# Attention to the memory by three one-pass products, with ScalarE scaling the probabilities

## The chip, the cores and the metric

The kernel runs on one core of a Trainium2 chip. The metric is the device time of one execution in microseconds; lower is better. Engines: PE (TensorE), DVE (VectorE), ACT (ScalarE), POOL (GpSimd) and SP (SyncE, which here only issues DMAs). Each engine works through its own instructions in the order in which they are written, and waits on semaphores.

## What is computed

Two transformer blocks in a row on 512 tokens of width 1024. The change touches one sublayer of the second block: attention from the tokens to a memory of 256 rows, with 4 heads of 256 channels.

```python
def memory_cross_attention(h, mem_n, w_mem_q, w_mem_kv, w_mem_o):
    q = jnp.einsum("bsd,de->bse", h, w_mem_q).reshape(B, S, MEM_HEADS, MEM_HEAD_DIM)
    kv = jnp.einsum("bmd,de->bme", mem_n, w_mem_kv)
    k = kv[..., :D_MODEL].reshape(B, M, MEM_HEADS, MEM_HEAD_DIM)
    v = kv[..., D_MODEL:].reshape(B, M, MEM_HEADS, MEM_HEAD_DIM)
    s = jnp.einsum("bshd,bmhd->bhsm", q, k).astype(jnp.float32) * (MEM_HEAD_DIM ** -0.5)
    p = jax.nn.softmax(s, axis=-1).astype(v.dtype)
    o = jnp.einsum("bhsm,bmhd->bshd", p, v).reshape(B, S, D_MODEL)
    return jnp.einsum("bse,ed->bsd", o, w_mem_o)
```

The rest of the two blocks (the projections, two other attentions, convolutions and two feed-forward parts) is the same before and after.

## The kernel before

**Products.** Nearly all matrix products are made of three one-pass products of float32r operands (`mm3`, L909 to L912): an operand is split into a high part and a remainder, and high x high, low x high and high x low are added up in the bank. POOL splits the weights slab by slab (`split`, L752 to L758: a high copy, L756, and the subtraction, L758, 128x2048 each). The high part of an activation is a copy by ACT out of the bank, its remainder a subtraction by DVE. A product of plain float32 operands is one call, which the trace shows as two instructions. In the attention to the memory the scores (`scoresm`, L1423) and the values (`valuesm`, L1441) are plain float32 products, and the transposes of the probabilities (`turnm`, L1432) are plain products with an identity.

**Staging.** The keys and values of the memory, `mem_k` and `mem_v`, are made in earlier parts of the kernel and copied out of their banks by ACT (L1588). They were computed from `mt_hi` and `mt_lo`, the split of the normalized memory, which nothing reads after that. The queries are projected in 8 banks, the first four in two halves of 256 tokens, the last four 512 wide from two slabs of weights; ACT copies each bank to `qm` (L1634, called at L1968) and thereby frees it. PE waits for all 8 banks (L1451) and for a DMA that brought back half of `mem_k` (L1452).

**The order of the stage.** `ATTM_ORDER` is written out by `head_order` (L224): z0, z1, t0, z2, t1, o0, z3, t2, o1, t3, o2, o3. Here z is a head's scores (4 tiles of 128 tokens by 256 keys), t its transposes (2 banks of 128 keys by 512 tokens), o its values (2 banks of 128 channels by 512 tokens). PE, ACT and DVE each walk through this same list. The 32 tiles go round the 8 banks in turn.

- DVE, at z (L2489 to L2501): for each of 4 tiles the maximum (L2494) and its product with minus the scale (L2495, through the helper at L2059); then for each tile the reciprocal of the sum (helper at L2065) and the product of the probabilities by it (L2501, also L2059). At o: the remainder of the head's output (`lo_of_head`, L2242, helper at L2050).
- ACT, at z (L1870 to L1878): for each tile the exponential with its sum (L1876), which frees the bank. At t: the copy of the transposed probabilities to `ptm` or `ptm_odd` (L1885), which frees the bank. At o: the high part of the output (`split_head`, L1673, at L1678).
- PE, at t, waits for DVE's probabilities (L1433), and at o for ACT's copies (L1442).

Before the stage ACT loads the table for the exponential (L1966). POOL splits the slabs of the query and output projections in one loop (L862). After the stage PE goes on with the output projection from `mem_o` (L1455).

Of the kernel before, what the change touches and what calls it, by code (L numbers as in the profile page):

```python
# [20 lines left out]
ALU = mybir.AluOpType  # L21
# [274 lines left out]
def build(nc, A, out):  # L296
    with ExitStack() as ctx:
# [3 lines left out]
        def sem(name):  # L301
            return ctx.enter_context(nc.semaphore(name))
# [98 lines left out]
        with ExitStack() as lend:  # L401
            dn_lo = sb("dn_lo", [P, 7, D], F32R, where=lend)
            p1_sum = sb("p1_sum", [P, 2, T], where=lend)
        mem_k = sb("mem_k", [P, DC, NM])
        mem_v = sb("mem_v", [P, MT, D])
        mt_hi = sb("mt_hi", [P, DC, NM], F32R)
# [25 lines left out]
        ph = ExitStack()  # L432
        qm = sb("qm", [P, DC, T], where=ph)
        pm = sb("pm", [P, 2, NT, NM], where=ph)
        ptm = sb("ptm", [P, MT, T], where=ph)
        gain5 = sb("gain5", [P, D], where=ph)
        ptm_odd = sb("ptm_odd", [P, MT, T], where=ph)
        ptm_of = (ptm, ptm_odd)
        ph.close()

# [298 lines left out]
        def _(g):  # L739
# [117 lines left out]
            for i in range(2 * NT * (PAIRS - POOL_PAIRS), 2 * NT * PAIRS):  # L857
# [3 lines left out]
                g.tensor_scalar(out, out, smx[:, 2, j, qt:qt + 1], 1.0, ALU.mult, ALU.mult).then_inc(sm_p_pool, 1)  # L861
            split_all(n, S0["ffn"] + 2)  # L862
            g.wait_ge(xn5_ready, NT)
# [29 lines left out]
        def _(pe):  # L893
# [9 lines left out]
            def slab(i=None, per=0):  # L903
# [3 lines left out]
                return n % RING  # L907

            def mm3(o, ah, al, bh, bl, start, stop):  # L909
                inc_free(pe.matmul(o, ah, bh, start=start, stop=False))  # L910
                pe.matmul(o, al, bh, start=False, stop=False)  # L911
                return pe.matmul(o, ah, bl, start=False, stop=stop)  # L912

# [509 lines left out]
            def scoresm(h):  # L1423
                for qt in range(NT):
                    t = Tile(TTM["z", h] + qt)
                    t.wait_free(pe)
                    for c in range(2):
                        ins = pe.matmul(t.ap[:, 0:NM], qm[:, 2 * h + c, qt * P:qt * P + P], mem_k[:, 2 * h + c, :],  # L1428
                                        start=c == 0, stop=c == 1)
                    ins.then_inc(t.full, 1)  # L1430
# [10 lines left out]
            def valuesm(h):  # L1441
                all_taken(range(TTM["t", h], TTM["t", h] + MT))  # L1442
                for c in range(2):
                    t = Tile(TTM["o", h] + c)
                    t.wait_free(pe)
                    for kc in range(MT):
                        ins = pe.matmul(t.ap[:], mem_v[:, kc, h * MHD + c * P:h * MHD + c * P + P], ptm_of[h % 2][:, kc],  # L1447
                                        start=kc == 0, stop=kc == MT - 1)
                    ins.then_inc(t.full, 1)

            all_taken(range(T0["mem_q"], T0["mem_q"] + DC))  # L1451
            pe.wait_ge(k_back, 16)  # L1452
            for what, h in ATTM_ORDER:
# [57 lines left out]
        def _(act):  # L1511
# [356 lines left out]
            def softmax_attention(order, tt, heads, keys, p_of, pt, scale, mb, out_of):  # L1868
                for what, h in order:
                    if what == "z":  # L1870
                        for qt in range(NT):
                            t = Tile(tt["z", h] + qt)
                            act.wait_ge(sm_max, mb + NT * h + qt + 1)
                            if h >= 2 and qt == 0:
                                Tile(tt["t", h - 2] + keys // P - 1).wait_full(act)
                            st.done(act.activation(p_of(h)[:, qt], t.ap[:, 0:keys], ACT.Exp, scale=scale(h, qt),  # L1876
                                                   bias=smx[:, 0, h % 2, qt:qt + 1],
                                                   accum_out=smx[:, 1, h % 2, qt:qt + 1]), tile=t)  # L1878
                    elif what == "t":
                        for kc in range(keys // P):  # L1880
                            t = Tile(tt["t", h] + kc)
                            t.wait_full(act)
                            if h >= 2 and kc == 0:
                                Tile(tt["o", h - 2] + len(out_of(h)) - 1).wait_full(act)
                            st.done(act.copy(pt[h % 2][:, kc], t.ap[:]), tile=t)  # L1885
                    elif what == "m":
                        memory_out(h)
                    else:
                        for c, n in enumerate(out_of(h)):
                            split_head(tt["o", h] + c, ht_hi, h if heads == H1 else None, n)  # L1890
# [74 lines left out]
            act.dma_start(gain5[:], A["norm_ffn_pre_2"].partition_broadcast(P)).then_inc(gain5_loaded, 16)  # L1965
            load_table(ACT.Exp)  # L1966
            for m in range(DC):
                copy_out(T0["mem_q"] + m, qm[:, m])  # L1968
            softmax_attention(ATTM_ORDER, TTM, MH, NM, lambda h: pm[:, h % 2], ptm_of, lambda h, qt: SCM, NT * H1,
                              lambda h: [2 * h, 2 * h + 1])  # L1970
# [71 lines left out]
        def _(v):  # L2042
# [442 lines left out]

            def softmax_attention(order, tiles, heads, keys, p_of, minus_scale, mb, ob, out_of, fill):
                seen = ob
                for what, h in order:
                    if what == "z":  # L2489
                        for qt in range(NT):  # L2490
                            t = Tile(tiles["z", h] + qt)
                            t.wait_full(v)
                            st.after()
                            do(v.tensor_reduce(smx[:, 3, h % 2, qt:qt + 1], t.ap[:, 0:keys], AX_X, ALU.max))  # L2494
                            ts(smx[:, 0, h % 2, qt:qt + 1], smx[:, 3, h % 2, qt:qt + 1], *minus_scale(h, qt), ALU.mult,  # L2495
                               ALU.mult, sem=sm_max)
                        for qt in range(NT):
                            fill()
                            Tile(tiles["z", h] + qt).wait_taken(v)
                            recip(smx[:, 2, h % 2, qt:qt + 1], smx[:, 1, h % 2, qt:qt + 1])  # L2500
                            ts(p_of(h)[:, qt], p_of(h)[:, qt], smx[:, 2, h % 2, qt:qt + 1], None, ALU.mult, sem=sm_p)  # L2501
                    elif what == "o":
# [51 lines left out]
            for c in range(CC):  # L2554
                v.wait_ge(part_hi, CC + DC + c + 1)
                tt(ht_lo[:, c], ay[:, c], ht_hi[:, c].bitcast(F32), ALU.subtract, part_lo)
            post_and_norm(lambda m: post_psum(2, m, T0["w_out2"]), "nt4", col(V_NMEM, 8), ht_hi, ht_lo)
            softmax_attention(ATTM_ORDER, TTM, MH, NM, lambda h: pm[:, h % 2], lambda h, qt: (-SCM, None), NT * H1, 2 * PAIRS,
                              lambda h: [2 * h, 2 * h + 1], lambda: None)
# [173 lines left out]
```

## Time and profile before

| | |
|---|---|
| timed runs | 1483.13 us median of 3 (1480.7 to 1483.78) |
| profiled execution | 1481.8 us |
| its span, first to last instruction | 1480.0 us |
| mean granted clock of PE over the span | 0.998 of full speed |
| PE busy | 1440.3 us, 97% |
| DVE, ACT, POOL busy | 833.5, 552.0, 988.7 us |

The trace is of one execution. Times in it are microseconds from the first instruction. In a row of the timeline or of a group, `out<-in` names the tile written and the tiles read, L is a line of the kernel (often that of a helper), `x16` is the number of instructions; what stands in square brackets, or after a bar, is the idle time of the engine just before and what ended it. Matmuls are pipelined, so the distance of their starts counts, not their durations. PEclk is the granted clock of PE as a share of full speed.

### The profile page before, as it was taken

To read this page: it belongs to the slowest core of one execution; us is meant where nothing else is said; L and a number is where in the kernel's file an instruction comes from. 1 tells how busy PE (TensorE), PEld (TensorE's weight loads), DVE (VectorE), ACT (ScalarE), POOL (GpSimd) and SP (SyncE) were. 2 spreads that over 40 slices of the span, in tenths; PEclk is the share of its full clock that TensorE was granted. 3 is DMA by queue.
4 is the path that set the end of the run, shared out by engine and by line. 5 is a ranking of instruction groups with operands and counts; after the bars stand their busy time and mean duration, and the time that the engine had idled before them with its cause. 6 is when DMAs were issued, how large, how long until landed. Compare 5 with 4: busy or idle time off the path is not lost.

```text
span 1480.0 us, 18618 instructions
## 1 busy us (share of the span) xinstructions
PE 1440.3 (97%) x6987; PEld 1169.2 (79%) x6987; DVE 833.5 (56%) x1302; ACT 552.0 (37%) x1075; POOL 988.7 (67%) x398
## 2 busy tenths in 40 slices
PE   3999999999999999999999999999999999999997
PEld 3888777778888888888898844789789888888886
DVE  6998144443665655566744786441516555465655
ACT  3201134332554434444333386452424523333214
POOL 1867454445678889888567995365154989788653
PEclk9999999999999999999999999999999999999999
DMA  9875221222543332322443200133024323232131
GB/s 346 301 269 211 100 85 58 86 105 95 173 143 111 114 114 93 107 98 73 156 136 100 85 1 1 63 130 122 1 86 143 114 87 113 86 114 86 58 98 73
DMA packets 103385, 167.88 MB, mean 113 GB/s; under 512 B 3917, under 2 KB 61185, under 8 KB 102785
## 3 DMA queue, kind: packets, MB, share of 16 engines
q1 hardware_dynamic: 100176, 160.45, 31.5%
q10 hardware_dynamic: 3121, 6.26, 1.3%
q8 instruction: 56, 0.92, 0.2%
q14 instruction: 32, 0.26, 0.1%
HBM read 161.97 MB, written 4.72 MB: 113 GB/s over the span
## 4 chain that ended last, share of the span: by engine, by line
PE 87%; DVE 8%; ACT 3%; DMA 1%; issue 1%; DVEq 0%; SPq 0%; ACTq 0%
PE bank L910 26%; PE bank L911 26%; PE bank L912 26%; DVE bank L2054 2%; DMA ada_w<-in_w_ada 1%; DVE smx L2514 1%; DVE x L2050 1%; PE bank L1371 1%; PE bank L1428 1%; PE bank L1447 1%; PE bank L1171 1%; DVE bank L2050 1%; ACT junk L1540 1%; PE bank L1194 1%; DVE facc L2050 1%
## 5 line engine op out<-in xcount | busy, mean ns | idle before, releaser
L910 PE MATMUL bank<-ht_hi,w_hi 128*128 128x512 f32 (+1 forms) x1200 | 442.7, 369 | 0.5 <-DVE ht_lo L2050 0.3
L912 PE MATMUL bank<-ht_lo,w_hi 128*128 128x512 f32 (+1 forms) x1200 | 440.0, 367 | 0.0
L911 PE MATMUL bank<-ht_hi,w_lo 128*128 128x512 f32 (+1 forms) x1200 | 440.0, 367 | 0.0
L758 POOL TENSOR_TENSOR w_lo<-w_raw,w_hi 128x2048 fp32r<-128x2048 f32 x83 | 388.7, 4683 | 6.9
L756 POOL TENSOR_SCALAR w_hi<-w_raw 128x2048 fp32r<-128x2048 f32 x83 | 162.3, 1955 | 340.8 <-DMA w_raw<-in_w_in 108.8
L910 PEld LDWEIGHTS bank<-ht_hi,w_hi 128*128 128x128 f32 x1200 | 226.4, 189 | 41.5 <-DVE ht_lo L2050 1.8
L912 PEld LDWEIGHTS bank<-ht_lo,w_hi 128*128 128x128 f32 x1200 | 226.4, 189 | 37.2
L911 PEld LDWEIGHTS bank<-ht_hi,w_lo 128*128 128x128 f32 x1200 | 226.5, 189 | 36.7 <-issue 0.5
L808 POOL TENSOR_TENSOR dn_lo<-dn_raw,dn_hi_all 128x1024 fp32r<-128x1024 f32 x77 | 184.8, 2422 | 49.3 <-ACT dn_hi_all L1738 49.2
L2054 DVE SCALAR_TENSOR_TENSOR uc<-bank,par,uc 128x511 f32<-128x511 f32 x88 | 66.0, 750 | 128.4 <-ACT uc L1992 125.2
L822 POOL TENSOR_TENSOR dn_raw<-dn_raw 128x1024 f32<-128x1024 f32 x44 | 105.9, 2408 | 18.1 <-DMA dn_raw<-in_w_mlp_out 7.3
L910 PE MATMUL bank<-w_hi,ht_hi 128*128 128x512 f32 x256 | 100.4, 392 | 0.2 <-DVE facc L2050 0.2
L1992 ACT ACTIVATE uc<-bank,par 128x512 f32<-128x512 f32 x44 | 34.4, 781 | 176.9 <-PE bank L912 176.8
L912 PE MATMUL bank<-w_lo,ht_hi 128*128 128x512 f32 x256 | 99.7, 389 | 0.0
L911 PE MATMUL bank<-w_hi,ht_lo 128*128 128x512 f32 x256 | 99.6, 389 | 0.0
L2050 DVE TENSOR_TENSOR facc<-bank,facc 128x512 f32<-128x512 f32 x120 | 83.0, 692 | 22.5 <-PE bank L912 14.3
L2054 DVE SCALAR_TENSOR_TENSOR ada_acc<-ada_w,cvec,ada_acc 128x1024 f32<-128x1024 f32 x42 | 79.4, 1890 | 8.3 <-DMA ada_w<-in_w_ada 4.5
L1738 ACT CAST dn_hi_all<-dn_raw 128x1024 fp32r<-128x1024 f32 x77 | 77.1, 1054 | 18.1 <-PE bank L912 15.2
L910 PE MATMUL bank<-dn_hi_all,hf_hi 128*128 128x512 f32 x176 | 68.6, 390 | 0.6 <-issue 0.5
L911 PE MATMUL bank<-dn_hi_all,hf_lo 128*128 128x512 f32 x176 | 68.5, 389 | 0.0
L912 PE MATMUL bank<-dn_lo,hf_hi 128*128 128x512 f32 x176 | 68.5, 389 | 0.0
L2050 DVE TENSOR_TENSOR bank<-bank,hr 128x512 f32<-128x512 f32 x32 | 22.4, 700 | 81.1 <-ACT hr L1751 80.3
(302 smaller groups left out, 2402.7 us busy)
## 6 DMA issues: line engine op xcount, KB each, us to landing
w_raw<-in_w_in SPq DMA_DIRECT2D x27, 1024.0 KB, 5.0
ada_w<-in_w_ada SPq DMA_DIRECT2D x48, 512.0 KB, 7.1
w_raw<-in_w_up SPq DMA_DIRECT2D x22, 1024.0 KB, 4.9
w_raw<-in_w_mlp_in SPq DMA_DIRECT2D x16, 1024.0 KB, 5.6
dn_raw<-in_w_mlp_out SPq DMA_DIRECT2D x28, 512.0 KB, 4.6
w_raw<-in_w_out SPq DMA_DIRECT2D x8, 1024.0 KB, 5.0
w_raw<-in_w_mem_kv SPq DMA_DIRECT2D x8, 1024.0 KB, 5.3
dn_raw<-in_w_down SPq DMA_DIRECT2D x16, 512.0 KB, 5.2
```

Source lines behind the costliest of these rows:

```text
L756: g.tensor_scalar(w_hi[:, r], w_raw[:, r], 1.0, 1.0, ALU.mult, ALU.mult).then_inc(slab_hi, 1)
L758: g.tensor_tensor(w_lo[:, r], w_raw[:, r], w_hi[:, r].bitcast(F32), ALU.subtract).then_inc(slab_split, 1)
L808: g.tensor_tensor(dn_lo[:, w], dn_raw[:, w], dn_hi(w).bitcast(F32), ALU.subtract).then_inc(dn_split, 1)
L822: g.tensor_tensor(dn_raw[:, o], dn_raw[:, a], dn_raw[:, b], ALU.subtract).then_inc(t_made, 1)
L910: inc_free(pe.matmul(o, ah, bh, start=start, stop=False))
L911: pe.matmul(o, al, bh, start=False, stop=False)
L912: return pe.matmul(o, ah, bl, start=False, stop=stop)
L1171: pe.matmul(t.ap[:, 0:W1[qt]], q1[o, p, qt * P:qt * P + P], k1[o, p, 0:W1[qt]], start=True, stop=True).then_inc(t.full, 1)
L1738: st.done(act.copy(dn_hi(w), dn_raw[:, w]), dn_cast)
L1992: st.done(act.activation(uc[:, c], tiles[c].ap[:], ACT.Identity, scale=par[:, p, 2 + g, k:k + 1], bias=par[:, p, 6 + g, k:k + 1]), uc_ready)
L2050: do(v.tensor_tensor(o, a, b, op), sem, tile)
L2054: do(v.scalar_tensor_tensor(out=o, in0=a, scalar=s, in1=b, op0=op0, op1=op1), sem, tile)
```

## The change

The scores and the values of the attention to the memory are computed by three one-pass products (`three`, which `mm3` now also calls). What this needs, and what goes with it:

- ACT casts `mem_k` and `mem_v` to high parts (into the space of `mt_lo` and `mt_hi`) right after the table load; POOL makes their remainders in place, between the third and the fourth slab of the query projection. PE waits for these remainders in place of the DMA.
- ACT writes the queries scaled, as a high part; DVE makes the remainder out of the bank and frees it.
- DVE writes the row maximum negated, in one instruction; the exponential has scale 1.
- DVE writes only the reciprocal of the sums; ACT multiplies the probabilities by it, after the four exponentials of a head.
- ACT's copy of the transposed probabilities is their high part; DVE makes the remainder and frees the bank (a new branch at t in its list).

```diff
@@ buffers @@
+        mem_k_lo = sb("mem_k_lo", [P, DC, NM], F32R)
+        mem_v_lo = sb("mem_v_lo", [P, MT, D], F32R)
...
+        mem_k_hi = mt_lo
+        mem_v_hi = mt_hi[:].rearrange("p (a b) n -> p a (b n)", a=MT)
@@ POOL @@
-            split_all(n, S0["ffn"] + 2)
+            split_all(n, S0["mem_q"] + 3)
+            g.wait_ge(kv_hi, 1)
+            g.tensor_tensor(mem_k_lo[:], mem_k[:], mem_k_hi[:].bitcast(F32), ALU.subtract).then_inc(kv_lo, 1)
+            g.wait_ge(kv_hi, 2)
+            g.tensor_tensor(mem_v_lo[:], mem_v[:], mem_v_hi.bitcast(F32), ALU.subtract).then_inc(kv_lo, 1)
+            split_all(S0["mem_q"] + 3, S0["ffn"] + 2)
@@ PE @@
+            def three(o, ah, al, bh, bl, start, stop):
+                first = pe.matmul(o, ah, bh, start=start, stop=False)
+                pe.matmul(o, al, bh, start=False, stop=False)
+                return first, pe.matmul(o, ah, bl, start=False, stop=stop)
...
-                        ins = pe.matmul(t.ap[:, 0:NM], qm[:, 2 * h + c, qt * P:qt * P + P], mem_k[:, 2 * h + c, :],
-                                        start=c == 0, stop=c == 1)
+                        q = slice(qt * P, qt * P + P)
+                        _, ins = three(t.ap[:, 0:NM], qm_hi[:, 2 * h + c, q], qm_lo[:, 2 * h + c, q],
+                                        mem_k_hi[:, 2 * h + c, :], mem_k_lo[:, 2 * h + c, :], c == 0, c == 1)
...
-                        ins = pe.matmul(t.ap[:], mem_v[:, kc, h * MHD + c * P:h * MHD + c * P + P], ptm_of[h % 2][:, kc],
-                                        start=kc == 0, stop=kc == MT - 1)
+                        d = slice(h * MHD + c * P, h * MHD + c * P + P)
+                        _, ins = three(t.ap[:], mem_v_hi[:, kc, d], mem_v_lo[:, kc, d], ptm_of[h % 2][:, kc],
+                                  ptm_lo[h % 2][:, kc], kc == 0, kc == MT - 1)
...
-            pe.wait_ge(k_back, 16)
+            pe.wait_ge(kv_lo, 2)
@@ ACT @@
+                        for qt in range(NT):
+                            act.wait_ge(pm_inv, NT * h + qt + 1)
+                            st.done(act.activation(p_of(h)[:, qt], p_of(h)[:, qt], ACT.Copy,
+                                                   scale=smx[:, 2, h % 2, qt:qt + 1]), sm_p)
...
-                            st.done(act.copy(pt[h % 2][:, kc], t.ap[:]), tile=t)
+                            st.done(act.copy(pt[h % 2][:, kc], t.ap[:]), ptm_made)
...
+            act.wait_ge(k_back, 16)
+            st.after()
+            st.done(act.copy(mem_k_hi[:], mem_k[:]), kv_hi)
+            st.done(act.copy(mem_v_hi, mem_v[:]), kv_hi)
             for m in range(DC):
-                copy_out(T0["mem_q"] + m, qm[:, m])
-            softmax_attention(ATTM_ORDER, TTM, MH, NM, lambda h: pm[:, h % 2], ptm_of, lambda h, qt: SCM, NT * H1,
+                t = Tile(T0["mem_q"] + m)
+                t.wait_full(act)
+                st.done(act.activation(qm_hi[:, m], t.ap[:], ACT.Copy, scale=SCM), qm_made)
+            softmax_attention(ATTM_ORDER, TTM, MH, NM, lambda h: pm[:, h % 2], ptm_of, lambda h, qt: 1.0, NT * H1,
@@ DVE @@
-                            do(v.tensor_reduce(smx[:, 3, h % 2, qt:qt + 1], t.ap[:, 0:keys], AX_X, ALU.max))
-                            ts(smx[:, 0, h % 2, qt:qt + 1], smx[:, 3, h % 2, qt:qt + 1], *minus_scale(h, qt), ALU.mult,
-                               ALU.mult, sem=sm_max)
+                            do(v.tensor_reduce(smx[:, 0, h % 2, qt:qt + 1], t.ap[:, 0:keys], AX_X, ALU.max, negate=True),
+                               sm_max)
...
-                            recip(smx[:, 2, h % 2, qt:qt + 1], smx[:, 1, h % 2, qt:qt + 1])
-                            ts(p_of(h)[:, qt], p_of(h)[:, qt], smx[:, 2, h % 2, qt:qt + 1], None, ALU.mult, sem=sm_p)
+                            recip(smx[:, 2, h % 2, qt:qt + 1], smx[:, 1, h % 2, qt:qt + 1], pm_inv)
+                    elif what == "t":
+                        for kc in range(MT):
+                            t = Tile(tiles["t", h] + kc)
+                            v.wait_ge(ptm_made, MT * h + kc + 1)
+                            tt(ptm_lo[h % 2][:, kc], t.ap[:], ptm_of[h % 2][:, kc].bitcast(F32), ALU.subtract, tile=t)
...
+            for m in range(DC):
+                v.wait_ge(qm_made, m + 1)
+                t = Tile(T0["mem_q"] + m)
+                stt(qm_lo[:, m], t.ap[:], SCM, qm_hi[:, m].bitcast(F32), ALU.mult, ALU.subtract, tile=t)
```

## Rows read from the trace of the kernel before

**Rows 1.** The page, engines: busy time, share of the span, instructions

```profile
PE 1440.3 (97%) x6987; PEld 1169.2 (79%) x6987; DVE 833.5 (56%) x1302; ACT 552.0 (37%) x1075; POOL 988.7 (67%) x398
```

**Rows 2.** Chain of waits, 1005 to 1090: start us, length us, engine, tile, line

```profile
1042.32 0.59 ACT qm L1634
...
1043.27 7.14 PE bank L1428 x32
1050.41 0.87 PE bank L1438 x8
1051.28 3.46 PE bank L1428 x16
...
1055.61 3.44 PE bank L1447 x8
...
1074.55 0.23 PE bank L910
```

**Rows 3.** Windows, the stage: length, each engine's busy us, PEclk, DMA

```profile
1043.00:1076.00 33.00, 32.73 (x135) 22.97 (x136) 21.79 (x72) 18.32 (x49) 0.26 (x1) 1.00 0.02 1
```

**Rows 4.** Timeline, PE: first and last of 52, then of 34: start, duration

```profile
1005.82 0.28 PE L912 MATMUL bank<-ht_lo,w_hi 128*128 128x256 f32 x1
...
1011.94 0.28 PE L912 MATMUL bank<-ht_lo,w_hi 128*128 128x256 f32 x1
...
1034.42 0.39 PE L912 MATMUL bank<-ht_lo,w_hi 128*128 128x512 f32 x1
...
1041.90 0.39 PE L912 MATMUL bank<-ht_lo,w_hi 128*128 128x512 f32 x1
```

**Rows 5.** Timeline, ACT: exp and copy of a head; the first copy of qm

```profile
1016.22 0.59 ACT L1634 COPY qm<-bank 128x512 f32<-128x512 f32 x1 [8.94 <-PE bank L912]
...
1052.35 0.47 ACT L1876 ACTIVATE pm<-bank,smx 128x256 f32<-128x256 f32 x1 [0.15 <-DVE smx L2059]
...
1052.82 1.06 ACT L1885 COPY ptm<-bank 128x512 f32<-128x512 f32 x2
```

**Rows 6.** Timeline, ACT elsewhere: products by a column, 128 and 512 wide

```profile
810.28 7.71 ACT L1854 ACTIVATE tap_m<-ident,vec 128x128 f32<-128x128 f32 x26
...
867.92 0.71 ACT L1909 ACTIVATE p2c<-p2c,smx 128x512 f32<-128x512 f32 x1
868.53 0.71 ACT L1909 ACTIVATE p2b<-p2b,smx 128x512 f32<-128x512 f32 x1
```

**Rows 7.** Timeline, DVE: product, reciprocal, two remainders, maximum

```profile
1052.62 0.35 DVE L2059 TENSOR_SCALAR pm<-pm,smx 128x256 f32<-128x256 f32 x1
1052.89 0.15 DVE L2065 RECIPROCAL smx<-smx 128x1 f32<-128x1 f32 x1
...
1059.11 1.49 DVE L2050 TENSOR_TENSOR ht_lo<-bank,ht_hi 128x512 fp32r<-128x512 f32 x2
1060.70 0.42 DVE L2494 TENSOR_REDUCE smx<-bank 128x1 f32<-128x256 f32 x1
```

**Rows 8.** Groups by shape, DVE, ACT: busy us, mean ns, idle before

```profile
L2054 DVE SCALAR_TENSOR_TENSOR ay<-bank,ay 128x512 f32<-128x512 f32 x4 | 2.8, 692 | 1.7 <-PE bank L1399 1.6
...
L1743 ACT CAST w_hi<-w_raw 128x2048 fp32r<-128x2048 f32 x14 | 26.9, 1919 | 12.6 <-DMA w_raw<-in_w_mlp_in 12.6
```

**Rows 9.** Timeline, POOL: splits around its idle time

```profile
1002.48 4.62 POOL L758 TENSOR_TENSOR w_lo<-w_raw,w_hi 128x2048 fp32r<-128x2048 f32 x1
...
1019.91 1.92 POOL L756 TENSOR_SCALAR w_hi<-w_raw 128x2048 fp32r<-128x2048 f32 x1 [12.81 <-DMA w_raw<-in_w_mem_q]
```

**Rows 10.** Timeline, a wait of PE on DVE at 1113 to 1115

```profile
1113.48 1.28 DVE L2054 SCALAR_TENSOR_TENSOR xn<-x,stat,gain 128x1024 f32<-128x1024 f32 x1
...
1115.23 1.91 PE L1084 MATMUL bank<-ident,xn 128*128 128x128 f32 x16
```

**Rows 11.** Timeline, PE, then its window (length, PE busy, PEclk, DMA), 171 to 180

```profile
171.52 3.63 PE L1128 MATMUL bank<-ones,ada_acc 128*128 128x1 f32 x32
...
174.00:180.00 6.00, 6.00 (x22) 0.72 0.43 125
```

More of the change, by code:

```diff
@@ L403, in build @@
             p1_sum = sb("p1_sum", [P, 2, T], where=lend)
-        mem_k = sb("mem_k", [P, DC, NM])
-        mem_v = sb("mem_v", [P, MT, D])
+        with ExitStack() as lend:
+            mem_k = sb("mem_k", [P, DC, NM], where=lend)
+            mem_v = sb("mem_v", [P, MT, D], where=lend)
+        mem_k_lo = sb("mem_k_lo", [P, DC, NM], F32R)
+        mem_v_lo = sb("mem_v_lo", [P, MT, D], F32R)
         mt_hi = sb("mt_hi", [P, DC, NM], F32R)
@@ L432, in build @@
         ph = ExitStack()
-        qm = sb("qm", [P, DC, T], where=ph)
+        qm_hi = sb("qm_hi", [P, DC, T], F32R, where=ph)
         pm = sb("pm", [P, 2, NT, NM], where=ph)
-        ptm = sb("ptm", [P, MT, T], where=ph)
+        ptm = sb("ptm", [P, MT, T], F32R, where=ph)
         gain5 = sb("gain5", [P, D], where=ph)
-        ptm_odd = sb("ptm_odd", [P, MT, T], where=ph)
+        ptm_odd = sb("ptm_odd", [P, MT, T], F32R, where=ph)
         ptm_of = (ptm, ptm_odd)
+        qm_lo = sb("qm_lo", [P, DC, T], F32R, where=ph)
+        ptm_lo = [sb(f"ptm_lo{i}", [P, MT, T], F32R, where=ph) for i in range(2)]
+        mem_k_hi = mt_lo
+        mem_v_hi = mt_hi[:].rearrange("p (a b) n -> p a (b n)", a=MT)
         ph.close()
@@ L473, in build @@
         squared, mlp_slab_hi, mlp_hi, mlp_sums = (sem(n) for n in ("squared", "mlp_slab_hi", "mlp_hi", "mlp_sums"))
+        qm_made, ptm_made, kv_hi, kv_lo, pm_inv = (sem(n) for n in ("qm_made", "ptm_made", "kv_hi", "kv_lo", "pm_inv"))
         memory_kept, mt_back, k_back = sem("memory_kept"), sem("mt_back"), sem("k_back")
@@ L907, in slab @@
                 return n % RING
+            def three(o, ah, al, bh, bl, start, stop):
+                first = pe.matmul(o, ah, bh, start=start, stop=False)
+                pe.matmul(o, al, bh, start=False, stop=False)
+                return first, pe.matmul(o, ah, bl, start=False, stop=stop)
             def mm3(o, ah, al, bh, bl, start, stop):
-                inc_free(pe.matmul(o, ah, bh, start=start, stop=False))
-                pe.matmul(o, al, bh, start=False, stop=False)
-                return pe.matmul(o, ah, bl, start=False, stop=stop)
+                first, last = three(o, ah, al, bh, bl, start, stop)
+                inc_free(first)
+                return last
             def wv(r, k):
@@ L2484, in _, with softmax_attention @@
             per_tile = -(-(DVE_CC * K2 - sum(TAPS_BEFORE_ROPE) - TAPS_BEHIND_K) // (H1 * NT))
-            def softmax_attention(order, tiles, heads, keys, p_of, minus_scale, mb, ob, out_of, fill):
+            def softmax_attention(order, tiles, heads, keys, p_of, mb, ob, out_of, fill):
                 seen = ob
@@ L2557, in _ @@
             post_and_norm(lambda m: post_psum(2, m, T0["w_out2"]), "nt4", col(V_NMEM, 8), ht_hi, ht_lo)
-            softmax_attention(ATTM_ORDER, TTM, MH, NM, lambda h: pm[:, h % 2], lambda h, qt: (-SCM, None), NT * H1, 2 * PAIRS,
+            for m in range(DC):
+                v.wait_ge(qm_made, m + 1)
+                t = Tile(T0["mem_q"] + m)
+                stt(qm_lo[:, m], t.ap[:], SCM, qm_hi[:, m].bitcast(F32), ALU.mult, ALU.subtract, tile=t)
+            softmax_attention(ATTM_ORDER, TTM, MH, NM, lambda h: pm[:, h % 2], NT * H1, 2 * PAIRS,
                               lambda h: [2 * h, 2 * h + 1], lambda: None)
```

## The prediction

> **What bounds the kernel now.** I read the page's engine line first: PE is busy 97% of the span, VectorE 56%, ScalarE 37% [rows 1], so an edit pays by the PE time that it takes away, as long as nobody keeps PE waiting. A busy PE is only an average, so next comes the chain of waits through the stage that the diff touches. From the last copy of the queries (1042.32) on, the chain is PE alone: scores L1428, transposes L1438 and values L1447 follow each other without a wait until the output projection's product at 1074.55 [rows 2]. The stage lasts 1074.55 - 1043.27 = 31.28 us, 2% of the span. The windows view says how much cover there is: in 33 us VectorE works 21.8 and ScalarE 18.3 [rows 3]. Neither is idle enough to take on any amount, and both work in a fixed order, so the question is whether they stay hidden.
>
> **The change on PE.** A score tile is two plain products before, six one-pass products after. A head's 4 tiles take 3.46 us now [rows 2]. The one-pass form 256 columns wide starts every (1011.94 - 1005.82) / 51 = 0.120 us, a weight load before each [rows 4], so a head takes 24 x 0.120 = 2.88. A head's two value tiles take 3.44 now [rows 2]; 512 wide the spacing is (1041.90 - 1034.42) / 33 = 0.2267 [rows 4], so 12 x 0.2267 = 2.72. The transposes stay at 0.87 a head [rows 2]. PE's own work falls from 31.28 to 4 x (2.88 + 0.87 + 2.72) = 25.9: 5.4 us less.
>
> **The start.** PE's first score waits until the last query bank has been read. Before: ScalarE's copy ends at 1042.91, PE starts at 1043.27, 0.36 later [rows 2]. After: ScalarE's scaled copy (taken at the same 0.59), a signal of 0.03 (PE's last product ends at 1041.90 + 0.39 = 1042.29, the copy starts at 1042.32 [rows 4, 2]), then VectorE's remainder. The nearest row, the same form with a constant scalar out of a bank, takes 0.692 [rows 8]. So PE starts 0.72 later. Bounds: 0.69 (no signal seen) and 0.84 (the scale dearer than the copy, by at most the 0.12 by which a product by a column, 0.71, exceeds the copy, 0.59 [rows 6, 5]).
>
> **Costed at nothing.** ScalarE's two casts of the keys and values, 128x2048 each: 2 x 1.92 [rows 8], in an idle time of 8.94 us before 1016.22 [rows 5]. POOL's two subtractions: 2 x 4.62, starting at 1007.3 + 1.9 = 1009.2, done near 1018.6; POOL sits idle from 1007.1 to 1019.91 for the next query slab [rows 9]. If that cover fails by d, the fourth query slab's split is late by d; it ends at 1019.91 + 1.92 + 4.6 = 1026.5, and PE's 48 products on it, 10.9 us, end at 1042.1 [rows 4] and so begin at 1031.2: 4.7 us more hide it. The wait for the low parts is met 24 us early. Every slab and its DMAs keep their place.
>
> **ScalarE and VectorE, laid out.** ScalarE's product by a column is new at 256 wide. At 128 the spacing is (7.71 - 0.39) / 25 = 0.293, at 512 it is 868.53 - 867.92 = 0.61 [rows 6]; between them, by width, 0.40. I take 0.40 and keep both ends. An exponential with its sum takes 1052.82 - 1052.35 = 0.47 before the next may start, a bank copy 0.48 (0.59 until its result is there) [rows 5]. VectorE: a maximum 0.42 [rows 7]; written negated, no row shows it; between 0.42 and 0.42 + 0.15 for a second pass over the column (the 0.15 of a 1-column operation [rows 7]); I take 0.42, 0.50 from one start to the next. A reciprocal takes 0.2 with its gap, a remainder 0.75 (two in 1.49) [rows 7].
> Per head ScalarE has 4 x 0.47 + 4 x 0.40 + 4 x 0.48 = 5.4 us and VectorE 4 x 0.50 + 4 x 0.20 + 4 x 0.75 = 5.8, both under PE's 6.47. But they alternate. Time 0 is the first score:
> - Tile 0 is full at 6 x 0.12 - 0.12 + 0.28 + 0.03 = 0.91, its maximum done at 1.33, exponential at 1.36. Head 0's exponentials run at PE's 0.72 until 3.99, its products until 5.59. Head 1: exponentials to 7.47, products to 9.07, the copy of head 0's first transposed bank done at 9.66.
> - VectorE now has head 0's two remainders of the transposed probabilities, 9.69 to 11.19, in front of head 2's maxima (they wait behind them in its queue). First exponential of head 2: 11.19 + 0.42 + 0.03 = 11.64.
> - From there to head 3: exponentials at VectorE's pace 3 x 0.50 + 0.47 = 1.97, products 1.60, copy 0.59, four remainders on VectorE (two of probabilities, two of head 0's output) 3.00, maximum 0.42, two signals: 7.64 us. PE needs 6.47 for a head, so this loop is the bound. First exponential of head 3: 19.28.
> - Head 3's last product ends at 22.95; PE turns it 0.47 later [rows 10], at 23.4, having had nothing to do for some 2.3 us.
> - VectorE, in its order: remainders of head 2 to 24.97, of head 1's output to 26.47, of head 3's probabilities to 27.91. PE: head 2's values from 25.3 to 28.0, head 3's from 27.91 + 0.36 = 28.27 to 28.27 + 2.72 = 31.0.
> Laid out by the same steps, the kernel before ends at 31.4 against its 31.28, so the method is good to a few tenths.
>
> **The sum.** The stage ends at 31.0 instead of 31.28, and starts 0.72 later: +0.45 us. The 5.4 us of PE are handed back to waits on ScalarE and VectorE. The profiled execution took 1481.8 us, so it would take 1482.3; the median of the runs shown, 1483.13, stands 1.3 above it, so I expect 1483.6 in the timed runs. Something over 0.2%, 3 us, can be told from no change. Ends: the product by a column enters 16 times in series, so each 0.1 us is 1.6 us: at 0.293 the sum is -1.3, at 0.61 it is +3.8; a negation that costs 0.15 adds about 1.0.
> The Trainium skill speaks against this part of the change (ScalarE: Activation LUTs, Rules for kernel authors): products belong on VectorE, not ScalarE. The trace agrees: VectorE's product takes 0.35, the next operation starting 0.27 after it [rows 7], against the 0.40 above. By that rule, with the products left on VectorE, its 4 x 0.50 + 4 x 0.47 + 4 x 0.75 = 6.9 us a head would be the loop instead of 7.64, and the stage would end some 1.9 us earlier than in my sum.
>
> **Rivals.**
> Cover holds: ScalarE and VectorE overlap better than their order on paper allows, PE stays the bound. Then 25.9 + 0.72 - 31.28 = -4.7: 1478.5. For it: both engines' sums are below PE's, and the trace has PE as the only bound. Against: the two queues' order is fixed, and the 7.64 needs no long instruction. 0.10.
> Slower, by ScalarE's product: it is the only term that enters 16 times in the loop. Costing as much at 256 as at 512 wide, 0.61, it gives +3.8: 1487; it decides from 0.56 on. For: a fixed part is large (128 wide already takes 0.293). Against: both widths lie on one slope. 0.12, with other costs of the loop that no row shows.
> Slower clock: between about 21.1 and 25.3 PE has only 8 transposes. After 3.63 us of one-column products, the granted clock averaged 0.72 over 6 us at 174, part of it at 1.2 GHz instead of 2.4 [rows 11]; that is 6 x 0.28 = 1.7 us of full-speed work lost. Here it would hit the last values, which end the stage: up to +2.2 in all, 1485.3, still under 3. The stage now runs at 1.00 [rows 3], and so far it has no such gap. 0.15. [...]
> No real change of form: if the three products cost as much as the plain form, PE would show it as time on its own lines; 0.120 and 0.2267 are measured on the same shapes [rows 4], so under 0.03.
>
> **Numbers.** Forecast as summed 0.60, clock 0.15, cover holds 0.10, ScalarE's product 0.12, rest 0.03. Faster by over 0.2% is the cover's 0.10 with a little of the lower end: 0.12. Slower is 0.12 and the clock's upper edge, runs scattering by 1.5 us: 0.18. The same: 0.70. The range takes the lower end of the product (-1.3, with the scatter), part of the way to the cover's 1478.5, and goes up to the 0.61 case: 1479.5 to 1487.
>
> **What would show it.** In the changed trace: one-pass products at 0.120 and 0.227 on the lines of the scores and values; PE idle in front of transposes and values, about 2 us before the last head's transposes, released by ScalarE; the first score some 0.7 us later; exponentials of heads 2 and 3 some 7.6 us apart; ScalarE's product near 0.49 with 0.40 spacing; POOL's two subtractions inside its idle time. A stage of 26 to 27 us with PE never waiting proves me wrong one way, one of 34 the other.

## The result and the profile after

The changed kernel takes 1484.68 us (median of 22 runs, 1480.58 to 1487.42), the kernel before 1482.91 us (22 runs beside them, 1479.04 to 1484.81): ratio 1.0018, 95% interval 1.0010 to 1.0025, so 1.5 to 3.7 us slower. The forecast was +0.45 us. The profiled execution of the changed kernel has a span of 1480.7 us against 1480.0.

The page of the changed kernel, engines: busy time, share of the span, instructions (answers to [rows 1]).

```profile
PE 1437.6 (97%) x7035; PEld 1172.6 (79%) x7035; DVE 845.0 (57%) x1286; ACT 561.1 (38%) x1093; POOL 1000.5 (68%) x400
```

PE's busy time fell by only 2.7 us, and at 97% the page doesn't tell the two kernels apart. The answer stands in the chain of waits through the stage (start us, length us, engine, tile, line; answers to [rows 2]).

```profile
1041.50 0.61 ACT qm_hi L1998
1042.13 0.70 DVE qm_lo L2084
1042.83 0.35 issue
1043.18 0.36 PE bank L923
1046.33 0.44 DVE smx L2524
1046.79 0.56 ACT pm L1896 x2
1047.35 1.59 ACT pm L1901 x4
1048.94 1.81 ACT pm L1896 x8
1050.76 1.60 ACT pm L1901 x4
1052.35 0.48 ACT ptm L1909
1052.85 0.70 DVE ptm_lo L2080
1053.65 0.70 DVE ptm_lo L2080
1054.44 0.44 DVE smx L2524
1054.90 2.15 ACT pm L1896 x8
...
1062.33 0.44 DVE smx L2524
1062.79 2.15 ACT pm L1896 x8
1064.93 0.52 ACT pm L1901 x2
1065.63 0.90 ACT pm L1901 x2
1066.58 1.97 PE bank L1457 x8
1068.61 0.76 PE bank L923
```

Before, PE followed PE without a wait. Now the chain runs over ScalarE (L1896 the exponentials, L1901 its products by the reciprocal, L1909 the copy) and VectorE (L2080 the remainders, L2524 the maxima), and PE comes back into it only for the last head's transposes and the values of head 2 behind them (1068.61). The first exponentials of heads 2 and 3 are 1062.79 - 1054.90 = 7.89 us apart.

PE's waits of over 0.15 us in the stage, from its timeline (start us, duration, line, form, and in brackets the idle time before and what ended it):

```profile
1043.18 0.36 PE L923 MATMUL bank<-mt_lo,qm_hi 128*128 128x256 f32 x1 [1.72 <-DVE qm_lo L2084]
1054.44 0.47 PE L923 MATMUL bank<-ptm,mt_hi 128*128 128x512 f32 x1 [0.60 <-DVE ptm_lo L2080]
1061.58 0.47 PE L923 MATMUL bank<-ptm_odd,mt_hi 128*128 128x512 f32 x1 [0.23 <-DVE ht_lo L2080]
1066.58 1.97 PE L1457 MATMUL bank<-ident,pm 128*128 128x128 f32 x8 [2.04 <-ACT pm L1901]
```

The gap of 2.04 us before the last transposes is released by ScalarE's product, and the 8 transposes behind it take 1.97 us instead of the 1.03 to 1.23 that eight take earlier in the stage. The windows view of the same kernel (columns as in [rows 3], PEclk third from the end) shows why:

```profile
1066.00:1070.00 4.00, 3.35 (x11) 2.72 (x12) 2.66 (x4) 3.42 (x8) 0.00 (x0) 0.58 0.00 0
```

The granted clock averages 0.58 over these 4 us, part of it at 1.2 GHz instead of 2.4.

**How the rest is measured.** Two lengths carry the comparison. The gap is from the start of the last query product to the start of the first score; the stage is from the first score to the start of the second product of the output projection. Before: 1043.27 - 1041.90 = 1.37 and 1074.62 - 1043.27 = 31.35. After: 1043.18 - 1041.07 = 2.11 and 1075.08 - 1043.18 = 31.90. So +0.74 and +0.55. A third piece was not in the forecast. PE's timeline of the changed kernel, in the MLP behind the stage:

```profile
1157.30 0.47 PE L923 MATMUL bank<-dn_hi_all,hf_hi 128*128 128x512 f32 x1 [0.44 <-POOL dn_lo L816]
```

Before, no wait of PE on GpSimd shows there. What comes late is a transfer: just before `dn_lo`, GpSimd splits a slab of `w_up`, and it waits for that slab to land. GpSimd's timeline before, after, and in e10_early_filled below:

```profile
1144.99 1.92 POOL L756 TENSOR_SCALAR w_hi<-w_raw 128x2048 fp32r<-128x2048 f32 x1 [8.15 <-DMA w_raw<-in_w_up]
...
1145.68 1.92 POOL L764 TENSOR_SCALAR w_hi<-w_raw 128x2048 fp32r<-128x2048 f32 x1 [8.42 <-DMA w_raw<-in_w_up]
...
1146.82 1.92 POOL L764 TENSOR_SCALAR w_hi<-w_raw 128x2048 fp32r<-128x2048 f32 x1 [9.81 <-DMA w_raw<-in_w_up]
```

In all twelve profiles PE's wait follows this one: PE has none where GpSimd waits 8.06 to 8.17 us, 0.2 at 8.23, 0.3 to 0.5 at 8.34 to 8.53, 1.61 at 9.63 and 1.76 at 9.81. What delays the slab, no run shows, so this piece may not belong to the change. The three pieces add up to 1.73 us.

### The profile page after: what moved, and what is told of

It reads as the page before. It is cut to its first block, busy times and chain, and to the rows that moved or that the text cites. A ratio compares the mean times of both kernels' runs of the same rounds, so it can differ in the third digit from the quotient of the medians.

```text
span 1480.7 us, 18736 instructions
## 1 busy us (share of the span) xinstructions
PE 1437.6 (97%) x7035; PEld 1172.6 (79%) x7035; DVE 845.0 (57%) x1286; ACT 561.1 (38%) x1093; POOL 1000.5 (68%) x400
## 4 chain that ended last, share of the span: by engine, by line
PE 84%; DVE 8%; ACT 4%; DMA 2%; issue 1%; POOL 1%; DVEq 0%; SPq 0%; ACTq 0%; POOLq 0%
PE bank L923 26%; PE bank L925 26%; PE bank L924 26%; DVE bank L2084 2%; DMA ada_w<-in_w_ada 1%; DVE x L2080 1%; DVE smx L2547 1%; PE bank L1389 1%; PE bank L1189 1%; DVE bank L2080 1%; ACT junk L1560 1%; PE bank L1212 1%; DVE ht_lo L2080 1%; DVE facc L2080 1%; PE bank L1200 1%
## 5 line engine op out<-in xcount | busy, mean ns | idle before, releaser
L2080 DVE TENSOR_TENSOR facc<-bank,facc 128x512 f32<-128x512 f32 x120 | 83.0, 692 | 22.5 <-PE bank L925 14.3
L2084 DVE SCALAR_TENSOR_TENSOR ada_acc<-ada_w,cvec,ada_acc 128x1024 f32<-128x1024 f32 x42 | 86.5, 2060 | 7.7 <-DMA ada_w<-in_w_ada 4.1
L2080 DVE TENSOR_TENSOR bank<-bank,hr 128x512 f32<-128x512 f32 x32 | 22.4, 700 | 80.6 <-ACT hr L1771 79.9
```

The costliest lines, as they stand in the source:

```text
L2080: do(v.tensor_tensor(o, a, b, op), sem, tile)
L2084: do(v.scalar_tensor_tensor(out=o, in0=a, scalar=s, in1=b, op0=op0, op1=op1), sem, tile)
```

## Experiments

**e1_on_vector: the products back on VectorE.** All else is as in the changed kernel.

```diff
-    act.wait_ge(pm_inv, NT * h + qt + 1)
-    st.done(act.activation(p_of(h)[:, qt], p_of(h)[:, qt], ACT.Copy, scale=smx[:, 2, h % 2, qt:qt + 1]), sm_p)
...
-    recip(smx[:, 2, h % 2, qt:qt + 1], smx[:, 1, h % 2, qt:qt + 1], pm_inv)
+    recip(smx[:, 2, h % 2, qt:qt + 1], smx[:, 1, h % 2, qt:qt + 1])
+    ts(p_of(h)[:, qt], p_of(h)[:, qt], smx[:, 2, h % 2, qt:qt + 1], None, ALU.mult, sem=sm_p)
```

> The changed kernel with the products by the reciprocal given back to VectorE (reciprocal and product in turn, as before the change). Stage here: from the start of the first score to the start of the second product of the output projection; 31.35 us before the change, 31.90 after it. Theory 'loop' (ScalarE's products stand in series between exponentials and copies): VectorE's own 6.9 to 7.2 us a head becomes the bound, the stage takes 30.3 +- 0.3, that is 1.6 less than after the change. Rival 'VectorE's queue is the bound whoever scales': putting 16 more operations on it makes the stage longer than 31.9, by up to 16 x 0.27 = 4.3. Start unchanged at about 2.1 us from the last query product to the first score in both. Timed: within 0.1% of the kernel before by the loop, over 0.2% slower by the rival.

Measured: 1482.26 us, ratio to the kernel before 1.0007 (0.9997 to 1.0017). The stage is 1072.70 - 1042.71 = 29.99 us, 1.9 less than in the changed kernel and at the lower edge of what was expected. VectorE's timeline, head 2 to head 3:

```profile
1053.78 2.01 DVE L2520 TENSOR_REDUCE smx<-bank 128x1 f32<-128x256 f32 x4
1055.88 0.16 DVE L2091 RECIPROCAL smx<-smx 128x1 f32<-128x1 f32 x1
1056.08 0.35 DVE L2085 TENSOR_SCALAR pm<-pm,smx 128x256 f32<-128x256 f32 x1
...
1057.73 1.48 DVE L2076 TENSOR_TENSOR ptm_lo<-bank,ptm_odd 128x512 fp32r<-128x512 f32 x2
1059.32 1.49 DVE L2076 TENSOR_TENSOR ht_lo<-bank,ht_hi 128x512 fp32r<-128x512 f32 x2
1060.91 2.01 DVE L2520 TENSOR_REDUCE smx<-bank 128x1 f32<-128x256 f32 x4
```

From maxima to maxima it is 7.13 us instead of 7.89, and VectorE has no pause in it: four maxima, four times a reciprocal and a product (0.46 together), four remainders. So the bound is no longer a loop over two engines but VectorE's own queue, as expected, and it is still longer than PE's 6.47. PE still waits 1.76 us before the last transposes.

**e2_on_pool: the products on GpSimd**, between two slabs of the output projection, where it has nothing to do. PE waits for its semaphore.

```diff
-    split_all(S0["mem_q"] + 3, S0["ffn"] + 2)
+    split_all(S0["mem_q"] + 3, S0["mem_o"] + 2)
+    for i in range(NT * MH):
+        out = pm[:, i // NT % 2, i % NT]
+        g.wait_ge(pm_inv, i + 1)
+        g.tensor_scalar(out, out, smx[:, 2, i // NT % 2, i % NT:i % NT + 1], 1.0, ALU.mult, ALU.mult).then_inc(sm_p_pool, 1)
+    split_all(S0["mem_o"] + 2, S0["ffn"] + 2)
```

> The changed kernel with the products by the reciprocal on POOL, between two slab splits, where POOL is idle through the whole stage. Theory 'loop': with the products off both engines the loop is shorter than PE's 6.47 us a head, the stage comes near PE's own 25.9: 26.9 +- 0.5; no gap of 2 us in front of the last transposes, and no stretch at half clock. Timed 3.5 to 4.5 us below the kernel before (ratio 0.997 to 0.9975). Rival 'VectorE's remainders are the bound': 12 to 16 remainders of 0.8 in the way whoever scales, the stage stays above 30. Rival for POOL: its product of 256 columns takes much longer than 0.42 (no row shows it; 512 columns take 0.69), then the transposes wait for it.

Measured: 1479.61 us, ratio 0.9984 (0.9974 to 0.9995), faster than both kernels, though the middle of the gain, 2.4 us, is less than the 3.5 to 4.5 expected. The stage is 1070.26 - 1043.38 = 26.88 us, as expected. GpSimd's timeline (last head) and PE's one wait behind the first score:

```profile
1061.63 1.84 POOL L879 TENSOR_SCALAR pm<-pm,smx 128x256 f32<-128x256 f32 x4 [4.52 <-DVE smx L2096]
...
1063.52 1.09 PE L1462 MATMUL bank<-ident,pm 128*128 128x128 f32 x8 [0.20 <-POOL pm L879]
```

A product is dearer here, 1.84 / 4 = 0.46, than on ScalarE, 0.40. But GpSimd is idle for 4.52 us before them and nothing else queues behind them, so ScalarE goes on to the next exponentials and copies meanwhile. The gap falls from 2.04 to 0.20 us. So the queue that a product stands in counts for more here than its own time. VectorE's maxima of heads 2 and 3:

```profile
1052.90 2.01 DVE L2525 TENSOR_REDUCE smx<-bank 128x1 f32<-128x256 f32 x4
...
1059.26 2.01 DVE L2525 TENSOR_REDUCE smx<-bank 128x1 f32<-128x256 f32 x4
```

They are 6.36 us apart, and VectorE works through all of it. That is just under PE's 6.47 a head, so less work on PE alone would now win little more.

**e3_plain_products: the other parts alone.** The kernel before, with scaled queries, negated maxima and ScalarE's products; the products of scores and values stay plain.

```diff
-    do(v.tensor_reduce(smx[:, 3, h % 2, qt:qt + 1], t.ap[:, 0:keys], AX_X, ALU.max))
-    ts(smx[:, 0, h % 2, qt:qt + 1], smx[:, 3, h % 2, qt:qt + 1], *minus_scale(h, qt), ALU.mult, ALU.mult, sem=sm_max)
+    do(v.tensor_reduce(smx[:, 0, h % 2, qt:qt + 1], t.ap[:, 0:keys], AX_X, ALU.max, negate=True), sm_max)
...
+    st.done(act.activation(p_of(h)[:, qt], p_of(h)[:, qt], ACT.Copy, scale=smx[:, 2, h % 2, qt:qt + 1]), sm_p)
...
-    copy_out(T0["mem_q"] + m, qm[:, m])
+    st.done(act.activation(qm[:, m], t.ap[:], ACT.Copy, scale=SCM), tile=t)
```

> The kernel before with only the softmax part of the change: queries scaled on leaving the banks, maxima written negated, ScalarE multiplies the probabilities; scores and values stay plain products, with no splits and no remainders. Theory 'loop': without the remainders on VectorE the loop is some 6.2 us a head, under PE's 7.83, so PE stays the bound: stage 31.35 +- 0.3, PE without waits, start 1.4 us as before, timed within 0.1% of before. Rival 'ScalarE's products cost time by themselves': 16 x 0.40 in PE's way, stage 32.5 to 37.

Measured: 1480.82 us, ratio 1.0001 (0.9990 to 1.0013). Gap 1.38, stage 31.36 us, and no wait of PE behind the first score. With plain products, which need no remainders and keep PE busy longer, ScalarE's products cost nothing.

**e8_split_unused: the splitting alone.** e3_plain_products with ScalarE's casts and GpSimd's subtractions added, results unused.

```diff
+    g.wait_ge(kv_hi, 1)
+    g.tensor_tensor(mt_lo[:], mem_k[:], mt_lo[:].bitcast(F32), ALU.subtract).then_inc(kv_lo, 1)
...
+    st.done(act.copy(mt_lo[:], mem_k[:]), kv_hi)
```

> As e3_plain_products (plain products, scaled queries, negated maxima, products by the reciprocal on ScalarE), with ScalarE's two casts and GpSimd's two subtractions for the keys and values added; their results are not used. Theory (these steps are hidden by idle time): same time as e3_plain_products within 0.3 us in the profile, stage 31.4 +-0.3, last query product not delayed. Rival (the three-product kernels' median lies 1 to 2 us above what their stages explain, because the splitting takes time elsewhere): 1 to 2 us slower than e3_plain_products, ratio to the kernel before 1.0008 to 1.0015, with a gap on TensorE that GpSimd releases.

Measured: 1481.82 us, ratio 1.0000 (0.9989 to 1.0010); gap 1.38, stage 31.36 us. GpSimd's timeline:

```profile
1009.06 4.61 POOL L865 TENSOR_TENSOR mt_lo<-mem_k,mt_lo 128x2048 fp32r<-128x2048 f32 x1
1013.64 4.61 POOL L868 TENSOR_TENSOR mt_hi<-mem_v,mt_hi 128x2048 fp32r<-128x2048 f32 x1
1019.59 1.91 POOL L757 TENSOR_SCALAR w_hi<-w_raw 128x2048 fp32r<-128x2048 f32 x1 [1.33 <-DMA w_raw<-in_w_mem_q]
```

The fourth query slab still waits 1.33 us for its own transfer, so the cover holds. The wait on dn_lo in the MLP is there too, 0.40 us, and not in e3_plain_products: GpSimd waits 8.42 us for the slab of `w_up` here and 8.06 there. That the splitting delays the slab isn't shown, for e6_pool_early below splits, and the slab comes after 8.17 us.

**e7_products_twice: the suspected cost doubled.** Four more products on ScalarE behind each head's four.

```diff
+    for qt in range(NT):
+        st.done(act.activation(spare(NT * h + qt), qm_hi[:, 0, 0:NM].bitcast(F32), ACT.Copy, scale=vec[:, V_CB:V_CB + 1]))
```

> The changed kernel with four more products by a column on ScalarE behind each head's four, 256 wide, from other data into space that nothing reads; they only take time. Loop theory: the last four of head 3 lie behind the signal that TensorE waits for, the others lie in the loop: heads 0 to 2 delay it by 4 x 0.40 = 1.6 us each as far as ScalarE has no idle time left there; the stage grows by 3 to 5 us to 35 to 37 us. Rival (cover holds, ScalarE's products are hidden): the stage stays within 0.5 us of 31.9.

Measured: 1492.04 us, ratio 1.0061 (1.0047 to 1.0075); stage 1085.74 - 1045.75 = 39.99 us, above the 35 to 37 expected. ScalarE's and PE's timelines:

```profile
1060.67 0.47 ACT L1901 ACTIVATE pm<-bank,smx 128x256 f32<-128x256 f32 x1 [1.60 <-DVE smx L2531]
...
1070.14 0.48 ACT L1901 ACTIVATE pm<-bank,smx 128x256 f32<-128x256 f32 x1 [2.23 <-DVE smx L2531]
...
1073.78 1.69 ACT L1909 ACTIVATE junk<-qm_hi,vec 128x256 bf16<-128x256 f32 x4
...
1077.56 0.76 PE L923 MATMUL bank<-ptm,mt_hi 128*128 128x512 f32 x1 [2.54 <-DVE ptm_lo L2087]
```

The loop is 1070.14 - 1060.67 = 9.47 us, 1.58 more than 7.89. Behind the first score, the first exponential of head 2 starts at 1060.67 - 1045.75 = 14.92 us, in the changed kernel at 11.72: 3.20 more, which is 8 x 0.40. The values of head 2 start 1077.56 - 1045.75 = 31.81 us after the first score, in the changed kernel 25.43 (the 1068.61 of the chain above): 6.38 more, which is 16 x 0.40. An earlier stretch at half clock (0.50 over 1060 to 1064) leaves both steps at whole products. All sixteen stand in series; my expectation took the last head's four as free, but its transposed copies queue behind them. The other 1.7 us came on PE behind it, at half clock: the windows 1076 to 1078 and 1078 to 1080 are granted 0.50.

**e4_filled_gap: products in PE's gap.** Eight products whose result is overwritten keep PE busy before the last head's transposes.

```diff
+    if h == MH - 1:
+        t = Tile(TTM["t", h])
+        t.wait_free(pe)
+        for _ in range(8):
+            pe.matmul(t.ap[:], mem_k_hi[:, 0, 0:P], qm_hi[:, 0], start=True, stop=True)
```

> The changed kernel with 8 extra products of 512 columns on PE in front of the last head's transposes, into the bank that these overwrite, to keep PE busy in its gap of 2 us (they compute nothing that is used). Granted clock in the last 10 us of the stage 1.00 instead of 0.58 over 4 us. Theory 'hidden': the slow stretch cost at most 0.1 us, since the last head's values wait for VectorE's remainders anyhow; stage 31.8 +- 0.15. Rival 'clock': the slow stretch is what the forecast of 31.0 missed; stage shorter by 0.7 to 1.7: 30.2 to 31.2.

Measured: 1483.61 us, ratio 1.0017 (1.0007 to 1.0026). The clock stays at 1.00 through the stage, which is 1077.64 - 1045.94 = 31.70 us: 0.2 less. Most of the half clock was hidden in the changed kernel: at full clock PE waits 0.94 us for VectorE's remainders behind these transposes, as its timeline shows here:

```profile
1071.38 0.47 PE L923 MATMUL bank<-ptm,mt_hi 128*128 128x512 f32 x1 [0.94 <-DVE ptm_lo L2085]
```

**e5_early_start: the wait before the first score.** PE asks for the query banks head by head.

```diff
     def scoresm(h):
+        all_taken(T0["mem_q"] + 2 * h + c for c in range(2))
...
-    all_taken(range(T0["mem_q"], T0["mem_q"] + DC))
```

> The changed kernel, but TensorE asks for the query banks head by head (two banks before each head's scores) instead of for all eight before the first score. Theory (the wait before the first score costs its full length): the gap between the last query product and the first score falls from 2.10 us to near 0, the stage from the first score to the second output-projection product stays at 31.9 +-0.3, since ScalarE and VectorE start on it as much earlier; the kernel ends 2.0 us earlier than the changed kernel. Rival (the loop of ScalarE and VectorE is bound by when these two engines come free from the last query bank, not by TensorE's start): the stage grows by what the gap loses, to 33.5 to 34, and the end moves by under 0.5 us.

Measured: 1481.95 us, ratio 1.0003 (0.9993 to 1.0012). The gap is 1043.49 - 1043.26 = 0.23 us, as the theory said; the stage is 1076.37 - 1043.49 = 32.88, between the two expectations. Its last transposes start 23.48 us after the first score, as in the changed kernel (23.40), so ScalarE and VectorE did start earlier. The extra microsecond lies behind them, where the windows view has:

```profile
1068.00:1072.00 4.00, 3.06 (x8) 2.42 (x8) 3.48 (x6) 1.94 (x5) 0.00 (x0) 0.63 0.00 0
1070.00:1074.00 4.00, 4.00 (x14) 3.16 (x13) 2.58 (x4) 0.96 (x2) 0.00 (x0) 0.69 0.00 0
```

This time the clock fell behind the transposes and took the values, not the wait.

**e10_early_filled: both, the early start and the filled gap.** The edits are those of e5_early_start and e4_filled_gap.

> e5_early_start with the 8 extra products of e4_filled_gap in TensorE's gap before the last head's transposes. If the half clock cost e5_early_start its extra 1.0 us: the clock stays at 1.00 from 1060 on, the stage is 31.7 to 31.9 instead of 32.88, and the kernel is about 1 us faster than e5_early_start in the profile. Rival (the extra 1.0 us comes from the earlier start, as ScalarE and VectorE come free late): clock 1.00, stage still 32.6 to 33.

Measured: stage 1074.84 - 1043.08 = 31.76 us with the clock at 1.00, so the 1.1 us of e5_early_start were the clock's. The time did not follow: 1483.77 us, ratio 1.0011 (1.0000 to 1.0022). In the MLP, PE waits 1.76 us for GpSimd's dn_lo, behind the slab of `w_up` that lands late (9.81 us, shown above); e4_filled_gap has the same, 1.61 us. Why it lands so late in both kernels with extra products was not tried.

**e9_again: the changed kernel once more, no edit.**

> The changed kernel once more, unchanged, to see where the half clock falls in another execution. In the profile of the change it came at 1066.3 and ended at 1069.8, before the last values; in e5_early_start it came 1 us later in the stage and the stage was 32.9 us instead of 31.9. If the clock falls at a fixed place of the stage, it lies within 0.3 us of 23.1 to 26.6 us behind the first score again and the stage is 31.9 +-0.15. If it moves between executions, the stage is anywhere from 31.9 to 32.9, longer the later the clock falls. Ratio to the kernel before 1.0005 to 1.0017.

Measured: 1482.31 us, ratio 1.0010 (1.0000 to 1.0020). The gap before the last transposes is the same, and the clock does not fall. PE's timeline, then the window that had 0.58 above:

```profile
1066.14 1.09 PE L1457 MATMUL bank<-ident,pm 128*128 128x128 f32 x8 [2.02 <-ACT pm L1901]
```

```profile
1066.00:1070.00 4.00, 2.92 (x16) 2.43 (x17) 3.00 (x5) 3.17 (x8) 0.00 (x0) 1.00 0.00 0
```

The stage is 1074.42 - 1042.73 = 31.69 us, below both expectations, which took a fall for certain. The fall is no property of the program alone: it came at two places of the stage in two kernels and not at all here. The shortest stage of this form is 31.69; the fall adds 0.2 to 1.2.

**e6_pool_early: GpSimd's products and the early start together**, the edits of e2_on_pool and e5_early_start.

> Products by the reciprocal on GpSimd, as in e2_on_pool, and the query banks asked for head by head, as in e5_early_start. If the two add up: gap before the first score near 0 (2.10 less), stage 26.9 +-0.5, so 2.1 us faster than e2_on_pool and some 5.8 us faster than the kernel before by the sum of the stages (ratio 0.996). If GpSimd is still busy with its weight slabs when the first reciprocals are there, the stage grows by up to 2 us and little is won over e2_on_pool.

Measured: 1476.81 us (6 runs), ratio 0.9962 (0.9948 to 0.9976), 5.6 us faster than the kernel before and the best of all. Gap 1040.88 - 1040.66 = 0.22, stage 1067.85 - 1040.88 = 26.97 us. GpSimd's slab ends 2.62 us before the first products:

```profile
1044.90 1.84 POOL L879 TENSOR_SCALAR pm<-pm,smx 128x256 f32<-128x256 f32 x4 [2.62 <-DVE smx L2096]
```

**All of them beside the kernel before.** Gap, stage and the wait on dn_lo are from the profiles, the sum is their difference to before (1.37, 31.35, none); the last column is the ratio's interval times 1482 us.

| kernel | gap | stage | wait on dn_lo | sum | measured difference, us |
|---|---|---|---|---|---|
| after | 2.11 | 31.90 | 0.44 | +1.7 | +1.5 to +3.7 |
| e9_again | 2.11 | 31.69 | 0.53 | +1.6 | 0 to +3.0 |
| e1_on_vector | 2.10 | 29.99 | 0.4 | -0.2 | -0.4 to +2.5 |
| e2_on_pool | 2.10 | 26.88 | 0.2 | -3.5 | -3.9 to -0.7 |
| e3_plain_products | 1.38 | 31.36 | none | 0.0 | -1.5 to +1.9 |
| e8_split_unused | 1.38 | 31.36 | 0.40 | +0.4 | -1.6 to +1.5 |
| e4_filled_gap | 2.10 | 31.70 | 1.61 | +2.7 | +1.0 to +3.9 |
| e5_early_start | 0.23 | 32.88 | 0.34 | +0.7 | -1.0 to +1.8 |
| e10_early_filled | 0.23 | 31.76 | 1.76 | +1.0 | 0 to +3.3 |
| e6_pool_early | 0.22 | 26.97 | none | -5.5 | -7.7 to -3.6 |
| e7_products_twice | 2.11 | 39.99 | 0.49 | +9.9 | +7.0 to +11.1 |

Every sum lies inside its interval, so nothing beside the three pieces is needed. The intervals are 2 to 4 us wide, though, and the pieces are from one profile each: another piece of 1 us can't be ruled out.

## Why the prediction was right, and where it was off

**The main reasoning held.** PE's saving was handed back to the loop over ScalarE and VectorE, and the time came out within the range. That the sign of the small rest was right is partly luck: the forecast was +0.45 between ends of -1.3 and +3.8. e2_on_pool shows it from the other side: with the products out of ScalarE's queue and everything else of the change kept, the stage falls from 31.90 to 26.88 us, near PE's own work of 25.9.

**The change on PE.** The new forms have the spacing that was taken from [rows 4]; e2_on_pool, with 26.88 us from end to end and 0.2 of waits, leaves little room for a dearer one. No real change of form is out.

**The start.** Forecast +0.72, measured +0.74. The scaled copy takes 0.60 like the plain one, and the remainder 0.69 as in [rows 8]. What the forecast did not ask is whether the wait was needed: e5_early_start removes it without touching anything else.

**Costed at nothing.** ScalarE's casts take 1.90 each and GpSimd's subtractions 4.63 each, from 1008.52 to 1017.7; GpSimd then still waits 1.38 us for the slab. e8_split_unused confirms it in the stage; the 0.4 us on dn_lo stays open.

**ScalarE and VectorE.** The product by a column, 0.40 by interpolation between [rows 6], starts every 0.40 (four in 1.69), and e7_products_twice shows that it enters 16 times in series. The negated maximum costs nothing extra (0.42). By the layout, head 2 would start at 11.64 us, head 3 at 19.28, the last transposes at 23.4 and the last values at 28.27 to 31.0; they came at 11.72, 19.61, 23.40 and, without the fall of the clock (e9_again), at 28.63 to 31.47. The terms that were mis-sized are the remainders, one every 0.80 us and not 0.75, and the pace of exponentials and maxima, 0.53 and not 0.50. So the loop is 7.89 and not 7.64 us. The rows had the 0.80: in [rows 7] the maximum starts 1060.70 - 1059.11 = 1.59 us after the first of two remainders, and 1.49 is only the time to the end of the second. That the last transposes come at 23.40, as forecast, is luck: by the chain above, ScalarE's last product ends at 1066.53, which is 23.35 and not 22.95, but PE starts 0.05 behind it and not the 0.47 taken from a wait of PE on VectorE [rows 10]. Two errors cancel.

**The sum.** The stage was forecast 0.28 shorter and came out 0.55 longer (0.34 without the fall of the clock). With the 0.44 on dn_lo, for which the forecast had no term, this makes +1.7 in place of +0.45, and the first timing, at 1.5 to 3.7, lies outside the forecast's value though inside its range. Same was given 0.70: the ratio's middle, 1.0018, lies just under 0.2%, and its interval reaches above.

**The rivals.** Cover holds: refuted for this order of the queues, and what it promised was to be had by moving one operation. ScalarE's product as the slower case: the mechanism is right, the price was the lower one. Slower clock: the fall was there, at the place named, and cost 0.2 us in the changed kernel because PE waits there for VectorE anyway; where it came later and took the values (e5_early_start) it cost 1.1. What went ahead of it differs from [rows 11], where PE had no gap but one-column products. The Trainium skill (TensorE: Matmul & The Clock Gate, Why this matters for your kernels) warns of idle gaps between bursts of products, though longer ones than here. The traces agree that a fall can follow a gap: with gaps of 2.04 and 2.00 us it came (after, e5_early_start), with 2.02 and 1.76 it did not (e9_again, e1_on_vector), and with the gap filled it stayed away in both profiles (e4_filled_gap, e10_early_filled).

**Where the products belong.** The Trainium skill (ScalarE: Activation LUTs, Rules for kernel authors) would have them on VectorE. e1_on_vector agrees, by 1.7 us of the stage against e9_again's 31.69; the timed runs of the two can't be told apart. The profile had a better place: the engine that was idle through the whole stage, at a higher price for each.

## What to carry to other kernels

When the bound engine's work is cut, lay out the other engines' queues in order: two engines that are each under the bound in sum can still form a loop that is over it, if they hand work to each other in a fixed order. Then a step is priced by the queue that it stands in, not by its own time. An idle engine with a dearer instruction (0.46 against 0.40 us) gave back 5 us here, and asking for two banks instead of eight was worth 2 more on top of that (e6_pool_early against e2_on_pool).

## What the runs showed of the hardware that was not expected

TensorE's clock in the same program falls in one execution and not in the next: in the changed kernel 0.58 over 1066 to 1070 in one, 1.00 in the other. The fall after the one-column products near 171 us, known from [rows 11], differs between profiles as well, though the edits lie far behind it. Windows of e9_again, then of e10_early_filled:

```profile
170.00:180.00 10.00, 10.00 (x48) 7.13 (x47) 6.04 (x11) 0.04 (x1) 0.48 (x1) 0.83 0.24 69
180.00:190.00 10.00, 10.00 (x46) 8.28 (x45) 0.24 (x4) 2.35 (x4) 6.54 (x2) 1.00 0.26 91
```

```profile
170.00:180.00 10.00, 10.00 (x42) 6.97 (x41) 4.75 (x10) 0.58 (x1) 1.25 (x1) 0.70 0.17 53
180.00:190.00 10.00, 10.00 (x44) 8.19 (x43) 1.53 (x6) 1.76 (x3) 4.46 (x2) 0.96 0.33 107
```

Eight profiles are of the first kind (0.83, then 1.00), four of the second (0.70 to 0.74, then 0.92 to 0.96: e4_filled_gap, e5_early_start, e7_products_twice, e10_early_filled). From the third group of PE's transposes at the start (near 27 us) to the last query product it is 1014.0 to 1014.8 us in the first kind and 1016.4 to 1016.9 in the second. The timed runs scatter with the clock too: of the 23 of the kernel before beside e9_again, the 12 with a mean granted clock of 0.998 or 0.999 average 1480.1 us, the 11 with 0.996 or 0.997 1483.4. None of this comes from the change: two single profiles of these kernels can differ by more than the change is worth, so stages were compared here, not spans.
